# Gate tiles of the next stage moved into the last pair of an attention, and four operations of another attention moved by a slot or so

## The reference

```python
y_b = dilated_attention(q, k, v) * jax.nn.silu(b_gate)            # first attention, 16 heads
g_a, g_b = jnp.split(jax.nn.sigmoid(gate_logits), N_BRANCHES, axis=-1)
merged = g_a * (y_a @ w_proj_a[layer]) + g_b * (y_b @ w_proj_b[layer])
...
# second attention, per block of queries
log_keep = jnp.where(strict, jax.nn.log_sigmoid(-z), 0.0)
suffix = lax.cumsum(log_keep, axis=3, reverse=True) - log_keep
weights = jnp.where(strict, jnp.exp(jax.nn.log_sigmoid(z) + suffix), 0.0)
outs.append(jnp.einsum('bhts,bhsd->bhtd', weights.astype(v.dtype), v[:, :, :kend]))
```

## Time and profile before

| | |
|---|---|
| median of 3 runs | 3405.32 us (3404.18 to 3412.97) |
| the profiled execution | 3399.16 us, span of its profile 3397.7 us |
| busy in the span | PE 3130.8 us (92%), DVE 1840.8, ACT 1404.4, POOL 667.5 |
| first attention | scores of its pairs begin at 563.61, 636.46, 709.30, 783.76, 858.22, 933.02, 1005.99, 1080.44 us |
| stage `pb` | first matmul at 1154.71 us, last one ends at 1321.76 us |
| second attention | scores of its pairs begin at 2511.92, 2595.19, 2678.77, 2762.80, 2847.99, 2931.57, 3015.16, 3097.89 us |
| a weight tile, 512 KB | median 3.5 us from issue to landing |
| half of y, 2 MB in one DMA | median 9.4 us from issue to landing |
| a low part of weights | DVE 1.22 us where nothing holds it, POOL 2.4 us |
| evacuation of half a dense tile on DVE | 0.69 us |

### The profile page before, as it was taken

One profiled execution on the slowest core, in us unless ns is written; L12 is line 12 of the kernel. 1 busy time (PEld: TensorE's weight loads), 2 busy tenths in 40 slices (PEclk: granted clock), 3 DMA queues, 4 the chain that ended last, 5 costly groups with the idle time before them and its releaser, 6 DMA issues. The chain is left out here.

```text
span 3397.7 us, 42014 instructions
## 1 busy us (share of the span) xinstructions
PE 3130.8 (92%) x15516; PEld 2609.2 (77%) x15516; DVE 1840.8 (54%) x2484; ACT 1404.4 (41%) x2100; POOL 667.5 (20%) x448
## 2 busy tenths in 40 slices
PE   6999999999999799879999999998889999997799
PEld 5788887888887587657777878777678888886677
DVE  4344223666666423356757566675447766776343
ACT  3333213555555422234334252434246666666331
POOL 3100002222222000211001020100224444443110
PEclk8999999999999899879999999999889999998899
DMA  2111222111111223002111121211211111111221
GB/s 96 41 48 41 74 68 72 59 57 57 57 59 67 75 70 109 32 27 71 53 58 56 50 75 44 75 44 62 82 32 38 38 38 38 38 38 44 113 73 56
DMA packets 54602, 197.36 MB, mean 58 GB/s; under 512 B 6304, under 2 KB 9248, under 8 KB 54176
## 3 DMA queue, kind: packets, MB, share of 16 engines
q1 hardware_dynamic: 45600, 164.66, 14.4%
q0 software_dynamic: 8832, 30.41, 2.9%
HBM read 165.56 MB, written 21.10 MB: 55 GB/s over the span
## 5 line engine op out<-in xcount | busy, mean ns | idle before, releaser
L114 ACT ACTIVATE whi<-wraw 128x1024 fp32r<-128x1024 f32 x208 | 218.4, 1050 | 451.3 <-PE a_D L127 59.2
L119 DVE TENSOR_TENSOR wlo<-wraw,whi 128x1024 fp32r<-128x1024 f32 x176 | 247.9, 1409 | 176.0 <-ACT whi L114 172.7
L125 PE MATMUL b_D<-x1hi,whi 128*128 128x512 f32 x640 | 255.9, 400 | 8.5 <-DVEq L999 6.6
L125 PE MATMUL ssm_D<-x1hi,whi 128*128 128x512 f32 x640 | 259.0, 405 | 4.6 <-DVEq L1748 4.6
L127 PE MATMUL ssm_D<-x1hi,wlo 128*128 128x512 f32 x640 | 252.0, 394 | 0.0
L126 PE MATMUL ssm_D<-x1lo,whi 128*128 128x512 f32 x640 | 251.9, 394 | 0.0
L126 PE MATMUL b_D<-x1lo,whi 128*128 128x512 f32 x640 | 251.3, 393 | 0.0
L127 PE MATMUL b_D<-x1hi,wlo 128*128 128x512 f32 x640 | 250.8, 392 | 0.0
L2178 DVE TENSOR_TENSOR_SCAN stick_keep<-stick_keep 128x896 f32<-128x896 f32 (+7 forms) x128 | 209.0, 1637 | 37.1 <-ACT stick_keep L2093 35.9
L125 PE MATMUL stick_D<-x1hi,whi 128*128 128x512 f32 x512 | 210.7, 412 | 7.0 <-DVE x1lo L152 7.0
L2321 POOL TENSOR_TENSOR stick_rows<-stick_rows,stick_keep 128x896 f32<-128x896 f32 (+7 forms) x128 | 157.9, 1236 | 295.2 <-DVE stick_keep L2178 290.1
(11 more groups left out here) (400 smaller groups left out, 8010.0 us busy)
## 6 DMA issues: line engine op xcount, KB each, us to landing
wraw<-w_dram SPq DMA_DIRECT2D x208, 512.0 KB, 3.5
sq<-acum_rows SPq DMA_DIRECT2D x32, 512.0 KB, 3.8
att_bias<-alibi_dram SPq DMA_DIRECT2D x16, 512.0 KB, 3.5
stack<-stack POOLq DMA_DIRECT2D x32, 256.0 KB, 3.6
x_sb<-xT_dram SPq DMA_DIRECT2D x8, 512.0 KB, 7.9
branch_a<-sq POOLq DMA_DIRECT2D x8, 512.0 KB, 3.5
y_b<-att_y POOLq DMA_DIRECT2D x8, 512.0 KB, 3.0
f<-y_b SPq DMA_DIRECT2D x2, 2048.0 KB, 9.4
```

The lines of the kernel that those rows point to most:

```text
L114: act.activation(self.whi[:, s, :, :], self.wraw[:, s, :, :], ACT.Copy).then_inc(self.w_hi, 1)
L119: dve.tensor_tensor(self.wlo[:, s, :, :], self.wraw[:, s, :, :], self.whi[:, s, :, :].bitcast(F32), ALU.subtract).then_inc(self.w_lo, 1)
L125: pe.matmul(out, self.whi[:, s, w0, :], xhi[:, k, cols], start=start, stop=False)
```

## The change

It has two parts, and data layout to go with them.

1. In the first attention the last pair does the full 64 units: the gate tiles 4 to 7 of stage `pb` stand in the places of k, q, v and gate. They are scaled into the tiles of k, q, v and the gate, and SP stores them to a new DRAM tensor `gates`. Behind the last pair PE does one more tile, the fifth of this kind, which stays in `b_D`. Stage `pb` begins with output tiles 4 to 7, for which only three gate products are left, and then does tiles 0 to 3 with gates that POOL loads back from DRAM; projection products of these alternate between two PSUM tiles and both weight slots. The first projection weights are split at the start of `pb`, no longer in the attention. The loops of `pb` are written out. Of eight gate tiles one ran in the attention before; five do after.
2. In the second attention, for all pairs but those where it says otherwise: DVE's split of the second weight tile (`split(p + 1, 1)`) goes from slot 0 to slot 1, behind the scan; ACT stores the second half of the turned k (`store_k`) in slot 11 behind the high parts of weights, and no longer at the end of slot 10; ACT's square of q and its split of the next pair's first weights go from slot 16 to slot 17, behind the high parts, and DVE's split of the same weights with them; POOL's `gain` of a tile for the pair after next goes from slot 8 to slot 11.

The state-space stage, with its six PSUM banks, is the same in both kernels.

```diff
 # first attention, SP
-                for p in range(PAIRS - 1):
+                for p in range(PAIRS):
                     pair(p)
 
                 sp.wait_ge(qk, 16 * (PAIRS - 1))
                 sp.wait_ge(y_left, 16 * (KT // 2))
                 sp.dma_start(y_first[:, 0:KT // 2, :], out[0:KT // 2].rearrange("k p t -> p k t")).then_inc(reloaded, 16)
+                for c, tile in enumerate((kT, qT, vT[:, :], gT[:, 0, :])):
+                    sp.wait_ge(evac, 8 * PAIRS + (2 * c + 4))
+                    sp.dma_start(gates[c, :, :], tile).then_inc(gates_left, 16)
                 sp.wait_ge(reloaded, 16)
+                sp.wait_ge(gates_left, 64)
...
 # first attention, PE
-                        n_units = UNITS[slot] if more else int(slot < 2 * KT)
-                        units(p + 1, u, u + n_units)
-                        u += n_units
+                        units(p + 1, u, u + UNITS[slot])
+                        u += UNITS[slot]
...
                 for p in range(PAIRS):
                     pair(p, p % 2, p < PAIRS - 1)
+                units(PAIRS + 1, 0, 2 * KT)
...
 # stage pb, POOL
+                pool.dma_start(loaded_gate[0], gates[0, :, :]).then_inc(g_land[0], 16)
+                for i in range(KT):
+                    pool.wait_ge(m_done, i + 1)
+                    pool.dma_start(part_a, spill[(HALF + i) % KT, :, :]).then_inc(a_land, 16)
+                    if HALF <= i < KT - 1:
+                        pool.dma_start(loaded_gate[(i + 1) % 2], gates[i + 1 - HALF, :, :]).then_inc(g_land[(i + 1) % 2], 16)
...
 # stage pb, PE
+                def late_tile(i):
+                    pe.wait_ge(K.w_lo, n0 + HALF + i + 1)
+                    if i == HALF:
+                        pe.wait_ge(g_scaled, HALF)
+                    else:
+                        pe.wait_ge(prod, i - 1)
+                    K.dense(pe, D2[:, :] if i % 2 else D[:, :], i % 2, yhi, ylo).then_inc(mm, 1)
...
 # stage pb, ACT and DVE, ahead of the split of y
+                K.split_hi(act, n0 // 2, 1)
...
+                K.split_lo(dve, n0 // 2, 1)
...
 # second attention, ACT
+                LATER = ("k_back1", "q_square")
...
+                        if more and slot == AUX_SLOT["k_back1"] + 1:
+                            store_k(p + 1, 1 - q, 1)
                         if slot < 16:
                             weights(p, q, slot)
...
+                            if slot == AUX_SLOT["q_sum"]:
+                                square_of(p + 1, 1 - q, 1)
+                                split(p + 2, 0)
                             aux(p + 1, 1 - q, slot)
-                        if more and slot == 16:
-                            split(p + 2, 0)
...
 # second attention, DVE
                     if slot == AUX_SLOT["q_sum"]:
+                        if p > 0:
+                            split(p + 1, 0)
                         inverse_q(p, q)
...
-                            if slot == 0:
+                            if slot == 1:
                                 split(p + 1, 1)
...
-                        if more and slot == 16:
-                            split(p + 2, 0)
...
 # second attention, POOL
-                        if more2 and slot in (8, 14):
+                        if more2 and slot in (11, 14):
                             gain(p + 2, int(slot == 14))
```

More of the change, by code:

```diff
@@ L567, in half_done_slot, with stage_attention @@
     return SLOT_OF[(2 * c + half) * KT + KT - 1]
-def stage_attention(K, D, xhi, xlo, stack, out, y_first):
+def stage_attention(K, D, xhi, xlo, stack, out, y_first, gates):
     nc, io = K.nc, K.io
@@ L632, in pair @@
                         K.load_weight(sp, n + 2, c % 2)
-                        if c % 2 == 1:
+                        if c % 2 == 1 and p < PAIRS - 1:
                             h = c // 2
@@ L703, in _ @@
                 for p in range(PAIRS):
-                    if p < PAIRS - 1:
-                        ahead(p + 1, (p + 1) % 2)
-                    else:
-                        split(p + 1, 1)
+                    ahead(p + 1, (p + 1) % 2, p < PAIRS - 1)
                     output(p, p % 2)
@@ L882, in pair @@
                                     high(p + 1, 1 - q, c)
-                        if more and slot == half_done_slot(2, 1) + 1:
+                        if slot == half_done_slot(2, 1) + 1:
                             split(p + 2, 0)
@@ L983, in pair @@
                             add_bias(p, slot)
+                        for c in range(4):
+                            for half in range(2):
+                                if half_done_slot(c, half) + 1 == slot:
+                                    scale(p + 1, 1 - q, c, half)
                         if more:
-                            for c in range(4):
-                                for half in range(2):
-                                    if half_done_slot(c, half) + 1 == slot:
-                                        scale(p + 1, 1 - q, c, half)
                             for h in range(2):
@@ L1021, in stage_pb @@
         gate, part_a = K.sq[:, 0, :], K.sq[:, 1, :]
-        y_hi, y_lo, y_land = sem("y_hi"), sem("y_lo"), [sem(f"y_land{k}") for k in range(KT // 2)]
+        loaded_gate = [K.acc[:, :], gate]
+        y_hi, y_lo, y_land = sem("y_hi"), sem("y_lo"), [sem(f"y_land{k}") for k in range(HALF)]
         mm, g_scaled, g_sig, prod, m_done, a_land = sem("mm"), sem("gs"), sem("sig"), sem("prod"), sem("merged"), sem("a_land")
+        g_land = [sem("g_land0"), sem("g_land1")]
         with nc.Block() as block:
@@ L1026, in _ @@
             def _(sp):
-                for k in range(KT // 2):
-                    sp.dma_start(y[:, KT // 2 + k, :], y_dram[KT // 2 + k, :, :]).then_inc(y_land[k], 16)
-                K.load_ahead(sp, "pb")
+                for k in range(HALF):
+                    sp.dma_start(y[:, HALF + k, :], y_dram[HALF + k, :, :]).then_inc(y_land[k], 16)
+                with sp.Fori(1, 7) as i:
+                    for s in range(2):
+                        sp.wait_ge(K.w_lo, 2 * i + (n0 + s - 1))
+                        K.load_weight(sp, 2 * i + (n0 + s), s)
@@ L1051, in _, with early_tile @@
-                tile(0, first=True)
-                with pe.Fori(1, KT) as j:
-                    tile(j)
+                def early_tile(i):
+                    pe.wait_ge(K.w_lo, 2 * i + (n0 + 2))
+                    if i >= 1:
+                        pe.wait_ge(prod, i)
+                    K.dense(pe, D2[:, :], 1, yhi, ylo, y_lo if i == 0 else None).then_inc(mm, 1)
+                def late_tile(i):
[5 more added lines that the diff above has]
+                    K.dense(pe, D2[:, :] if i % 2 else D[:, :], i % 2, yhi, ylo).then_inc(mm, 1)
@@ L1055, in _, with early_tile @@
+                for i in range(HALF):
+                    gate_tile(i)
+                    early_tile(i)
+                for i in range(HALF, KT):
+                    late_tile(i)
             @block.scalar
             def _(act):
-                def tile(j):
-                    act.wait_ge(g_scaled, j + 1)
+                def early_tile(i):
+                    act.wait_ge(g_scaled, i + 1)
                     act.activation(gate, gate, ACT.Sigmoid).then_inc(g_sig, 1)
                     for s in range(2):
-                        act.wait_ge(mm, 2 * j + s + 1)
-                        K.split_hi(act, j + (n0 // 2 + 1), s)
+                        act.wait_ge(mm, 2 * i + s + 1)
+                        K.split_hi(act, i + (n0 // 2 + 1), s)
@@ L1086, in _ @@
                 dve.sem_inc(m_done, 1)
+                K.split_lo(dve, n0 // 2, 1)
                 for k in range(KT):
                     K.tile_lo(dve, ylo, yhi, y, k, None, y_hi, y_lo)
-                with dve.Fori(0, KT) as j:
-                    tile(j)
+                for i in range(HALF):
+                    early_tile(i)
+                for i in range(HALF, KT):
+                    late_tile(i)
 def stage_residual(K, name, src, xhi, xlo, f_sb, x_dram, src_dram=None):
@@ L2055, in aux @@
                     for step, when in AUX_SLOT.items():
-                        if when == slot and step in AUX:
+                        if when == slot and step in AUX and not (p > 0 and step in LATER):
                             AUX[step](p, q)
```

93 lines of the change are left out of this document (52 added, 41 removed).

## The result

The changed kernel takes 3346.77 us (median of 4 runs, 3343.89 to 3352.10) against 3405.07 for the kernel before (median of 4): ratio 0.9825, 95% interval 0.9809 to 0.9841, 58.3 us faster. The forecast was 3353.7 with a range of 3341 to 3370.

The account below looks back on a forecast made before the run. TensorE, busy 92% of the span, was taken as the bound. Part 1's 32.5 us and part 2's 19.1 give 51.6 off 3399.16, so 3347.6; the median lies 6.2 us above: 3353.7, range 3341 to 3370.

Parts of the forecast that it names:

- Rival (d): First attention's last pair grows by the full 32.7 us of three tiles, to 94.8; gain 8, total 3379; chance 0.03.
- Rival (c): First attention to projection: y loads, barrier and half clock take their upper bounds; gain only 24 us, total 3362; chance 0.11.
- the tile of y: Projection's start: the tile ahead of the first gate tile, 12.5 us, ending 16.1 us behind the barrier.
- Both chains: Projection's start: weight split, first matmul and tile (16.1 us behind barrier); y's last tile to first gate tile (18.4 us).
- wait 1: Second attention: PE waits 1.77 us for POOL's product of row 1; forecast to stay, with 1.5 us gained over six pairs.
- (a): Second attention: POOL gets its product in ahead of VectorE's split, 0.85 to 1.7 us x 6 more; 3344; chance 0.16.
- (b): Second attention: put-off VectorE or ACT work holds PE instead, so 5 us stay of 19; 3367; chance 0.13.
- (e): Second attention: later split delays the fourth weight tile's load, POOL's gain product and row products; 3416 or more; chance 0.01.
- Waits 3 and 4: Second attention, slots 11 and 17: PE waits 0.81 and 0.72 us for low parts; forecast gain 12.2 us over seven pairs.
- wait 2: Second attention: PE waits 0.65 us for POOL's product of row 9, behind VectorE's scan; forecast gain 5.4 us over six pairs.

Follow-up runs that it names:

- part 1 alone: The changed kernel with all operations of the second attention where they were before: 3377.78 us against 3407.02 for the kernel before (ratio 0.9909).

## Why the prediction was right

**Part 1** came out by its own steps, by the trace (columns: forecast, measured):

| step | forecast | measured |
|---|---|---|
| last pair | 69.9 | 70.19 |
| fifth tile | 10.9 | 10.99 |
| PE's end to the barrier | 0.7 | 0.3 |
| barrier to the first gate tile | 18.4 | 18.0 |
| ten tiles | 108.9 | 109.1 |
| sum | 208.8 | 208.6 |

That a steady pair less what only a successor needs is the last pair, and not the old last pair plus three tiles, holds to 0.3 us. Rival (d), where the tiles are not hidden, would have given 94.8 us. Rival (c), a seam late enough to leave 24 us, is out. Inside the 18.0 us one step was off without harm: y's last tile came 11.1 us behind the barrier, 1.1 later than before and not 1.5, and the tile of y took 14.0 us (14.05 busy in its row) and not 12.5, as its first 14 matmuls ran at half clock. Both chains end in the same place: the gate tile waited 0.40 us for VectorE's low part.

**Part 2** gave 24.0 us in the profiled pair lengths, and 19.1 were forecast. The mechanisms were right: waits 2, 3 and 4 are gone and each by the move that was named; wait 1 stays with 1.44 us, POOL's product took 2.83 us where "near 3" was written, and one slot more frees it. Rivals (a), (b) and (e) are out: wait 1 did not close, no other wait appeared from the second pair on, and no pair is longer. The terms of the sum that were mis-sized:
- Waits 3 and 4 were taken at 0.87 + 0.88 = 1.75 us a pair and measured 2.13. Taken back one at a time, the store costs 1.18 and the square 0.96. The 0.16 us of overlap that I added to each idle row is too little: the first matmuls behind a wait also start further apart. In the rows above, 2732.83 to 2733.05 is 0.22 us for a step that takes 0.12 in a run. This is 0.1 for each wait, 0.2 of the excess of 0.38; the 0.1 us that I left on wait 3 is another, as no wait is left there. The rest, some 0.08 a pair, I can't place.
- Wait 1 was taken at 0.25 us in six pairs and measured 0.31 to 0.33, less a new 0.8 (0.64 of row and the overlap) once in the first pair, which the forecast had not seen; wait 2 was taken at 0.90 and measured 0.87.
- No term at all stood for the clock. Pair by pair the gain is 2.76 in the first, 3.33, 3.78, 4.98, 3.33, 3.35 and 2.48 (the last has no wait 2): the 4.98 holds a whole spell of 1.6 us and the 3.78 a longer wait 2. Another execution can hold more spells: with all four waits the seven pairs sum to 585.97 and 591.76 us (kernel before, part 1 alone), against 561.8 to 562.3 in the four kernels that have exactly the change's moves. So part 2 is worth 24 to 30 us by execution.

**The total.** The forecast for the profiled execution was 3347.6 and it took 3352.1; for the median it was 3353.7, and it is 3346.8. That both are so near is in part luck. The steps in error pull against each other: part 2 brought 4.9 us more than forecast, and the stages between the projection and the second attention, where I had nothing, took 10.4 more. And I added 6.2 us to get from the profiled execution to the median, where after the change the median lies 5.3 us below the profiled execution. The stages in between run the same work, before and then after (the columns of the earlier trace rows):

```profile
1321.76:2511.92 1190.16, 1084.74 (x5045) 879.15 (x5045) 692.79 (x870) 424.67 (x623) 143.66 (x88) 0.95 0.18 59
```

```profile
1289.20:2489.72 1200.52, 1091.60 (x5044) 882.98 (x5045) 692.30 (x870) 424.67 (x623) 145.98 (x88) 0.94 0.18 58
```

Of the 10.4 us, 6.9 are PE's busy time, with the same matmuls at a lower mean clock, and 3.5 are idle time. By stage they are 1.1 in `out`, 0.1 in `dt`, 3.7 in `ssm`, 2.9 in `ple0`, 0.7 behind it and 1.9 ahead of the first pair of `stick`. Two places show how the clock does it: PE has waited, and the spell of half clock there lies on more or fewer matmuls. The same 7 us of stage `ple0`, 40.2 us from its start, before and after, behind a wait of 2.0 and of 3.0 us:

```profile
2340.43:2347.43 7.00, 7.00 (x31) 5.80 (x32) 4.51 (x4) 3.14 (x4) 0.00 (x0) 1.00 0.25 74
```

```profile
2312.72:2319.72 7.00, 7.00 (x19) 5.51 (x20) 4.55 (x4) 3.13 (x4) 0.00 (x0) 0.57 0.26 78
```

31 matmuls against 19 is 2.7 us there; stage `out`'s first 16.6 us have a clock of 0.82 after and 0.90 before, 1.3 us. The 3.7 us of `ssm` I did not follow up. The difference is partly of the execution and partly of the change: over this stretch the five profiled kernels with the old projection took 1190.2 to 1193.7 us (mean 1192.0), the eight with the new one 1193.5 to 1200.9 (mean 1197.8). The two groups overlap by a hair: the 1193.5 is of the run with the store of k moved back, whose stage `out` has the clock of before (0.91). So some 6 us of part 1's 32.7 seem to be given back later, which is compatible with the 29.2 us that part 1 alone brought. Each figure is one execution of each kernel, and what in the new projection shifts the spells was not found; this stays open. That the medians nevertheless differ by 58.3, as much as the two stretches together (56.7), fits a profiled execution before with fewer spells in its pairs than the usual one has; the times of the other executions are known, their stages not.

## What to carry to other kernels

Cost work that moves under an existing stage by that stage's full period, and subtract what the full period holds beyond it, not by adding the work to the short one. Count the instructions that an in-order engine issues ahead of what the bottleneck waits for, and look for idle time of that engine one slot on: here the change's moves in the second attention and two more were worth some 50 us (27.4 alone, and 24 by the medians), with no work removed. And price a short wait of TensorE by the pair's length and not by its row: the row of 0.72 us cost 0.96, and 1.6 to 3.2 more where a spell of half clock followed.

## What the runs showed of the hardware

- A wait of TensorE of 0.72 us with 16 two-column matmuls behind it is followed, in one to five pairs of seven by kernel, by 3.4 us at the lower clock (0.52 in the row; 1.6 us lost) and twice by double that. A wait of 0.81 us with ordinary matmuls behind it is not (six pairs of six), nor are the two-column matmuls without a wait ahead of them (the changed kernel's pairs two to seven). In the first attention a wait of 1.76 to 2.11 us is, in two to four pairs of seven by kernel, and the one of 0.78 us in none.
- Where these spells fall differs between the profiled executions in stages that are the same in all kernels. Stage `ple0`, with the same instructions, took 122.0 to 124.9 us.
- A scan of 1024 columns on VectorE takes 2.29 us, and 3.43 us when POOL's gain product started first. A POOL product of 1024 columns takes 2.00 us, and 2.83 when VectorE's split started 0.23 us ahead of it; the split takes 1.20 us, and 2.27 when the product started 0.81 us ahead of it.
